# Layer 1's attention as one pipeline of 72 tiles, with queries made inside the pair ahead

## What is computed

```
z = rmsnorm(x, kv_norm) @ w_kvf                  # K, V (4 heads of 64), 16 gates
q = rmsnorm(x, attn_norm[1]) @ w_q               # 16 heads of 64
c = cumsum(log_sigmoid(gates))
s = q k^T / 8 + c[query] - c[key], causal
y = softmax(s) v @ w_o;   x = x + y
u = rmsnorm(x, ffn_norm) @ w_in                  # then the ConvFFN
```

## Time and profile before

| | us |
|---|---|
| median of 3 runs | 3716.15 |
| lowest and highest | 3711.89, 3719.15 |
| the profiled execution | 3712.74 |
| its span, first to last instruction | 3710.9 |
| mean granted PE clock of it | 0.934 |

### The profile page before, as it was taken

One profiled execution on the slowest core, in us unless ns is written; L12 is line 12 of the kernel. 1 busy time (PEld: TensorE's weight loads), 2 busy tenths in 40 slices (PEclk: granted clock), 3 DMA queues, 4 the chain that ended last, 5 costly groups with the idle time before them and its releaser, 6 DMA issues.

```text
span 3710.9 us, 53153 instructions
## 1 busy us (share of the span) xinstructions
PE 3387.5 (91%) x19257; PEld 3160.5 (85%) x19257; DVE 2230.0 (60%) x3542; ACT 1211.4 (33%) x2579; POOL 684.3 (18%) x289
## 2 busy tenths in 40 slices
PE   7999999999899999999898677878789999999997
PEld 5878888788799999999897577767679999999997
DVE  6444454544765666556767675666676665566575
ACT  3331323323422221222422556464642221222242
POOL 1002111111121221222232010101012222222131
PEclk7878898888899999999999898999999999999998
DMA  3111101111011111111112010101011111111111
GB/s 109 36 31 41 37 27 35 31 41 37 18 46 41 46 40 45 42 43 46 48 41 54 20 28 15 32 7 32 7 29 46 41 46 46 41 46 43 55 36 59
DMA packets 227310, 145.04 MB, mean 39 GB/s; under 512 B 34852, under 2 KB 208372, under 8 KB 226964
## 3 DMA queue, kind: packets, MB, share of 16 engines
q1 hardware_dynamic: 164792, 107.34, 9.8%
q10 hardware_dynamic: 62300, 34.62, 3.2%
HBM read 124.51 MB, written 17.42 MB: 38 GB/s over the span
## 4 chain that ended last, share of the span: by engine, by line
issue 44%; PE 44%; POOL 5%; DVE 4%; ACT 1%; DMA 1%; ACTq 0%; POOLq 0%; DVEq 0%
PE ps L454 13%; PE ps L456 12%; PE ps L455 12%; POOL t L429 4%; PE ps L568 2%; PE ps L589 2%; POOL t L425 2%; PE ps L542 1%; DVE t L1331 1%; DVE t L1542 1%; DVE t L1321 0%; DVE t L1305 0%; DVE t L1525 0%; PE ps L616 0%; PE ps L855 0%
## 5 line engine op out<-in xcount | busy, mean ns | idle before, releaser
L454 PE MATMUL ps<-t,t 128*128 128x384 f32 (+3 forms) x5144 | 1754.6, 341 | 85.8 <-DVE t L1295 25.4
L456 PE MATMUL ps<-t,t 128*128 128x384 f32 (+3 forms) x5144 | 1714.0, 333 | 0.0
L455 PE MATMUL ps<-t,t 128*128 128x384 f32 (+3 forms) x5144 | 1713.0, 333 | 0.0
L454 PEld LDWEIGHTS ps<-t,t 128*128 128x128 f32 (+1 forms) x5144 | 985.3, 192 | 166.9 <-DVE t L1321 48.0
L456 PEld LDWEIGHTS ps<-t,t 128*128 128x128 f32 (+1 forms) x5144 | 988.9, 192 | 7.7
L455 PEld LDWEIGHTS ps<-t,t 128*128 128x128 f32 (+1 forms) x5144 | 989.8, 192 | 3.2
L429 POOL TENSOR_TENSOR t<-t,t 128x1024 fp32r<-128x1024 f32 x205 | 535.0, 2610 | 1284.5 <-ACT t L1110 1278.6
L1295 DVE TENSOR_TENSOR t<-t,ps 128x384 f32<-128x384 f32 x720 | 365.2, 528 | 242.0 <-PE ps L456 239.8
L425 POOL TENSOR_TENSOR t<-t,t 128x1024 fp32r<-128x1024 f32 x75 | 148.7, 1983 | 1684.5 <-PE ps L456 1664.2
L954 ACT ACTIVATE t<-ps,t 128x128 f32<-128x128 f32 (+8 forms) x288 | 213.0, 740 | 426.4 <-DVE t L1388 406.0
L1388 DVE TENSOR_REDUCE t<-ps 128x1 f32<-128x128 f32 (+8 forms) x288 | 217.8, 756 | 219.0 <-PE ps L568 187.3
(11 more groups left out here) (142 smaller groups left out, 2915.8 us busy)
## 6 DMA issues: line engine op xcount, KB each, us to landing
t<-in_w_ffn_in SPq DMA_DIRECT2D x88, 512.0 KB, 3.9
t<-in_w_ffn_out SPq DMA_DIRECT2D x44, 512.0 KB, 3.8
t<-in_w_qkv_a SPq DMA_DIRECT2D x24, 512.0 KB, 3.8
out<-t ACTq DMA_DIRECT2D x24, 512.0 KB, 3.3
t<-in_w_ple_gate SPq DMA_DIRECT2D x16, 512.0 KB, 3.9
t<-in_x_prompt ACTq DMA_DIRECT2D x8, 512.0 KB, 7.8
t<-in_w_o_a SPq DMA_DIRECT2D x8, 512.0 KB, 4.0
t<-in_w_q_b SPq DMA_DIRECT2D x8, 512.0 KB, 4.0
```

Of the source, the lines that this page charges most:

```text
L454: pe.matmul(out, a_hi, b_hi, start=start, stop=False, skip_group_check=True)
L455: pe.matmul(out, a_hi, b_lo, start=False, stop=False, skip_group_check=True)
L456: return pe.matmul(out, a_lo, b_hi, start=False, stop=stop, skip_group_check=True)
```

## The change

It rewrites layer 1 from the K projection to the output projection, and one detail of both FFNs.

1. **One normalising.** K's normalising is done without a gain. POOL multiplies the chunks of `w_kvf` and `w_q` by their gains (`weigh`), ahead of the high and low parts. The first query chunk follows V's directly.
2. **Keys split once.** ACT and DVE make high and low parts of the keys as they come (`keys_high`, `kk_low`; the cached keys are turned by PE then too), SP stores them to DRAM (two arrays of 128 x 1600 for each two key heads), with the gates' two parts. SP loads the wanted rows for each pair, in an early and a late part. V's halves are made by POOL (`split_values`).
3. **One pipeline.** The 8 pairs of 9 tiles are one sequence of 72 rounds and two more, written out without a loop (`TILES_B`, `turned_at`). In round n the scores are of tile n, the turning is of tile n - 2, also across pairs. There is no drain but the last.
4. **Queries** of pair U + 1 are projected inside pair U, two or three of 24 steps a round behind the second scores (`queries_b`, `FILL`), all into bank 7. Every third round (t = 2, 5, 8) ACT and DVE take a segment at the round's end, and POOL copies it to `q_pick`. What picks the gates' rows no longer changes from pair to pair and is written once.
5. **Scaling** of both maps goes from DVE and ACT to POOL (`scale`).
6. **Outputs.** Bank 6 alone holds them. ACT copies the upper half for both heads in one instruction (`output_top`), DVE adds the lower (`output_sum`); both stand ahead of a later group's rounding and subtraction. POOL splits each segment, SP stores it to DRAM and loads all of it back in pair 7, in place of `h_hi` and `h_lo`. After the pipeline `w_o` is one run of eight `column_jobs`.
7. **FFN.** The down-projection's `row_jobs` and `add_rows` use five banks (3 to 7).

```diff
-        ("B", 4 * B_CHUNKS, 4 * B_JOBS),
+        ("B", B_CHUNKS, B_JOBS),
+KV_TURNS, T_KVF = [0, 4, 8, 11], 14
+UNITS, TILES_B = 8, 72
+def finished(k):
+    if k < 2 or held(k - 2):
+        return None
+    n, _ = TURNS[k - 2]
+    return n if k - 2 == TURN0[n + 1] - 1 else None
+def turned_at(n):
+    return range(TURN0[n - 2], TURN0[n - 1]) if 2 <= n < TILES_B + 2 else range(0)
...
 # SP
+            for U in range(UNITS):
+                b_chunk(U + 3)
+                if U == 7:
+                    sp.wait_ge(chunk_done, cb + 8)
+                    ...
+                    for V in range(6):
+                        load_output(V)
+                if U % 2 == 0 and U < 6:
+                    sp.wait_ge(v_split, U // 2 + 1)
+                    ...
+                    head_values(U // 2 + 1)
+                if U:
+                    store_output(U - 1, 2)
+                if U < 7:
+                    sp.wait_ge(s_done, scored(9 * U + 7, 1))
+                    keys_part(U + 1, 0, TP, early_loaded)
+                    store_output(U, 0)
+                    sp.wait_ge(s_done, scored(9 * U + 8, 1))
+                    keys_part(U + 1, TP, NK, late_loaded)
+                    store_output(U, 1)
...
 # POOL
+            def weigh(c, gain):
+                slot = c % 2
+                pool.wait_ge(w_loaded[slot], 16 * (c // 2 + 1))
+                pool.wait_ge(chunk_done, c - 1)
+                rows = w_raw[slot].rearrange("p (k n) -> p k n", n=P)
+                pool.tensor_tensor(rows, rows, gains[:, gain:gain + KT].unsqueeze(2).broadcast_to([P, KT, P]),
+                                   ALU.mult).then_inc(w_gained, 1)
+            def scale(n):
+                w, c = width_b(n), 2 * (n % 4)
+                pool.wait_ge(rz_done, 72 + n + 1)
+                for m, scaled in enumerate((scaled0, scaled1)):
+                    probs = p_b[n % 3][m][:, 0:w]
+                    pool.tensor_tensor(probs, probs, rz[:, c + m:c + m + 1].broadcast_to([P, w]), ALU.mult).then_inc(scaled, 1)
+            for n in range(TILES_B + 1):
+                U, t = divmod(n, 9)
+                if n:
+                    scale(n - 1)
+                if t == 0 and U:
+                    if U < UNITS:
+                        pair_queries(U, 2)
+                    split_output(U - 1, 1)
+                ...
+                if t == 1 and U < 6:
+                    weigh(c, G_ATTN + 8)
+                if t == 2 and U % 2 == 0 and U:
+                    split_values(U // 2)
+                if t == 3:
+                    if U < 7:
+                        pair_queries(U + 1, 0)
+                    ...
+                    round_up(c)
+                if t == 4 and U:
+                    split_output(U - 1, 2)
+                if t == 5:
+                    take_rest(c)
+                if t == 6 and U < 7:
+                    pair_queries(U + 1, 1)
+                if t == 7:
+                    split_output(U, 0)
...
 # PE
+            FILL = (0, 2, 5, 8, 11, 14, 16, 19, 21, 24)
+            for n in range(TILES_B + 2):
+                U, t = divmod(n, 9)
+                turns = turned_at(n)
+                if n < TILES_B:
+                    scores_b(n, 0)
+                for k in turns[0:2]:
+                    turn_b(k)
+                if n < TILES_B:
+                    scores_b(n, 1)
+                if U < UNITS - 1:
+                    queries_b(U + 1, FILL[t], FILL[t + 1])
+                for k in turns[2:]:
+                    turn_b(k)
...
-                            if j >= 4 or always:
-                                pe.wait_ge(freed, jobs_before(j - 3))
+                            if j >= banks or always:
+                                pe.wait_ge(freed, jobs_before(max(j - banks + 1, 0)))
...
 # ACT
-            norm_high(4, at["K"][0] + 5)
+            for n in range(TILES_B + 2):
+                ...
+                turn(turns[0:1])
+                if n < TILES_B:
+                    exponentials_b(n, 0)
+                turn(turns[1:2])
+                if n < TILES_B:
+                    exponentials_b(n, 1)
+                turn(turns[2:])
+                if U < UNITS - 1 and t % 3 == 2:
+                    queries_high(U + 1, t // 3, 7)
...
 # DVE
+            dve.wait_ge(kk_stored, 64)
             dve.memset(k_gates[64:P, :].bitcast(F32), 0.0).then_inc(gates_cleared, 1)
+            ...
+            for m in range(2):
+                p = dve.tensor_copy(q_pick[64:P, m, :], pick[64:P, m:m + 1].broadcast_to([64, T]))
             keep_kv(3)
+            for n in range(TILES_B + 2):
+                ...
+                if n < TILES_B:
+                    maximum_b(n, 0)
+                ...
+                turn(turns[0:2])
+                if n < TILES_B:
+                    maximum_b(n, 1)
+                turn(turns[2:])
+                if U < UNITS - 1 and t % 3 == 2:
+                    queries_low(U + 1, t // 3, 7)
```

784 lines of the change are left out of this document (424 added, 360 removed).

## The result

The changed kernel takes 3563.32 us (median of 4 runs, 3560.12 to 3571.75), the kernel before beside it 3714.02. The ratio is 0.9596, 95% interval 0.9574 to 0.9617: about 150 us or 4% less. The forecast was 3566 us, with 149 us less.

What follows compares the result with a forecast made beforehand. A DVE-ACT chain, no engine full, bounds layer 1's attention. 2060 + 425 (attention) + 98 (projection) + 8 = 2591 against 2719.1, 128 less; FFNs 21 less; 3712.7 - 149 = 3563.5, median 3.4 above: 3566 us; range 3500 to 3622.

Steps and rivals of the forecast that it cites:

- the alternation of DVE and ACT: Layer 1's attention: a chain of maximum, exponential, rounding and subtraction across both engines sets the pace, 53 us a pair.
- The rounds for which I named PE as last: Attention rounds t = 2, 3, 4: PE finishes last with scores, turning and queries, at 4.7, 4.0 and 4.4 us.
- Maxima that wait for PE: Attention: DVE's maxima waiting for PE would show the forecast to be wrong.
- t = 5: Attention round of 7.7 us: DVE waits for ACT's query rounding, and its next maximum is queued behind the query subtractions.
- 1.9 us for 1024 columns: POOL's scaling in the attention, priced from a one-operand form at 1.89 us; POOL's work 39 to 40 us a pair.
- The rival of a dear multiplication: POOL's scaling in the attention: at 3.4 us for 1024 columns the whole gain is gone; chance of slower 0.04.
- PE's work: Attention: 43 us a pair summed from its parts, 51 by the earlier busy time; PE is not last.
- One bank for the queries: Rival, attention: PE waits for DVE at the queries' bank, pairs stay at 59.5 us, 52 more, 3618; chance 0.09.
- Ahead of the attention: Layer 1 before the scores: they start at 2060 us, not 2076.1, with bounds 2048 and 2068.
- The two key splits: DVE work added ahead of the attention, about 2 x 2.8 us.
- Output projection and DRAM: After the attention: 4 x 24.5 = 98 us; the DRAM round trip costs nothing, 10 us if its cover is missing.
- the wait in the place forecast: Both FFNs: a fifth bank cuts PE's waits for DVE's additions from 12.7 to about 2.5 us an FFN, 21 us together.

Runs made afterwards that it cites:

- the run with two products: The changed kernel with two of the three products of the queries' jobs, the one with the activations' low part left out: 3564.0 us, ratio 0.9592.

## Why the prediction was right, and where its steps were off

**The bound.** That the alternation of DVE and ACT, not an engine's work, sets the pair was the step on which 425 us rested. It held for most of the pair: 53.7 us in the mean against 53, and 428.3 against 425 in all. POOL's work halved left the pair alone, PE's work cut by 2 us took 0.13 off it, and orders of the same instructions inside the rounds moved it between 50.7 and 54.4. In one round the limit is PE after all (t = 4, below).

**Round by round** (pairs 2 to 7, mean, forecast in brackets): 5.26 (5.3), 5.59 (4.6), 4.40 (4.7), 2.65 (4.0), 5.83 (4.4), 8.08 (7.7), 6.69 (6.8), 7.74 (7.8), 7.42 (7.7). The wide rounds, worked out link by link, are within 0.4. The rounds for which I named PE as last (t = 2, 3, 4) were wrong in size, 1.4 too much at t = 3 and 1.4 too little at t = 4, and right in their sum (12.9 for 13.1), which was luck. By the run with two products PE was the right ground for t = 4, which fell by 0.50, and the wrong one for t = 3, which fell by 0.05. Maxima that wait for PE were named as a sign of being wrong; in pairs 2 to 7 they stand behind t = 4 and, in every second pair, t = 3, nine waits of 0.7 to 1.2 us. At t = 1 a term was missing: in every second pair, where the key head changes, the last values of the pair before are held back to the round's end, and there it takes 6.3 us instead of 4.9.

**t = 5** went as described. DVE waits 1.93 us for ACT's query rounding, and the next maximum stands behind the subtraction. The timeline of DVE in the changed kernel:

```profile
2226.99 0.95 DVE L1690 TENSOR_REDUCE t<-ps 128x1 f32<-128x768 f32 x1
2229.86 1.12 DVE L1675 SCALAR_TENSOR_TENSOR t<-ps,t 64x384 fp32r<-64x384 f32 x2 [1.93 <-ACT t L1264]
2231.02 1.09 DVE L1690 TENSOR_REDUCE t<-ps 128x1 f32<-128x896 f32 x1
```

**POOL.** 1.9 us for 1024 columns was taken from another instruction of one operand, and it is 1893 ns; POOL's work is 36.9 us a pair, not 39 to 40, 69% and not 75% of the time. The rival of a dear multiplication had its price wrong: it scaled all of POOL's 40 us, though only the 22 of the scaling would grow, so the gain would be gone at about 4.6 us for 1024 columns (1.89 x (71.6 - 18)/22), not at 3.4. The price worked out from the Trainium skill's "GPSIMD Engine Reference", section 3, would have given 45; the trace doesn't bear it out for this form. The Trainium skill's rule in "SBUF — State Buffer", "Who interferes with whom", that DVE with one SBUF input and POOL don't get in each other's way, is confirmed by the trace: 35.6 us of DVE work a pair with POOL at 19.8, 36.9 and 47.1 us.

**PE's work** was put between 43 and 51; it is 46.4 in the mean of pairs 2 to 7. PE waits 68 us in the attention for DVE and ACT.

**One bank for the queries.** By this rival a pair would have stayed at 59.5 us. PE waits for the bank (L705 for L1675) 10.3 us in 14 times over seven pairs, 1.5 us a pair, where the rival needed 6.5.

**Ahead of the attention** 103.8 us against 108.8. DVE's last gate step ended at 2019.8 us, 80 behind the normalising's start, where 87 was counted (2038 - 1951.2). The two key splits took 3.51 and 4.63 us, not 2.8 each, so that term was 2.5 too small and the others together over 9 too large. Up to 4.5 us of that stands in the traces: three of DVE's gate steps ran beside POOL's subtractions before and were counted at that length, 2.90, 3.92 and 2.67 us, and take 1.27, 2.54 and 1.21 now (the hardware section has the rows of the first). The 1.6 us of the first lie ahead of a wait for PE of 4.13 us, so they may not count. How the rest divides (waits, first keys' store, the work counted ahead of the gate steps) no run took apart. From there to the first scores it was 23.6 us for 22.

**Output projection and DRAM.** 95.1 us for 98, PE busy in all of it (95.10 of 95.10). It starts right behind the last values. The outputs come back from DRAM in a burst, with the last load issued at 2445.4 us; here is DMA of the changed kernel in 40 slices of 2400 to 2475 us (busy tenths, then GB/s):

```profile
DMA  0005000000079989999999604993000000000000
GB/s 0 9 0 199 11 5 0 9 4 0 0 231 271 274 304 388 416 416 429 417 397 406 260 36 53 378 363 79 0 0 0 0 0 0 9 0 0 0 0 0
```

The last bytes land in the 28th slice, before 2453 us, and PE wants them at 2471.7. So the round trip cost nothing, as taken, though for 20 us it filled the DMA engines, where I had reckoned with a share of 0.24. That it costs nothing is read from the trace; no run took it away.

**FFN.** 20.0 us for 21, and the wait in the place forecast, 12.7 to 2.3 us.

**The whole.** The spans differ by 152.8 us against 149 forecast. 11.6 us of it lie ahead of the normalising: about 10 are the first FFN's banks, and the rest is within what identical code varies by (below). That the median came within 3 us of the forecast is in part luck: 5.0 us too much ahead of the attention and 2.9 in the output projection stand against 3.3 too little in the attention and 1.0 too much expected of the FFNs, and identical code varies by more than any of these.
